# Moving the root spreads, the decay sums and their exponentials among the projection tiles of a two-layer hybrid trunk, and waiting for a bank at the third Z tile alone

## What is computed

```python
z = h @ w_in                       # one combined projection, split into
qa, ka, va, ub, vb, qkvc, bc, ac, zc, gates = jnp.split(z, split_idx, axis=-1)
o_b = chunk_gmlp(gelu(ub), gelu(vb), ...)     # vb is RMS-normalised over its 512 columns
# mixer C, gated DeltaNet
q = l2norm(q) * DN_DK ** -0.5; k = l2norm(k)  # after a short conv and silu
g = -exp(a_log) * softplus(a_raw + dt_bias)
gc = cumsum(g)                                # in chunks of 64; exp(gc), exp(g_last - gc), exp(g_last)
o = rmsnorm(o_f + flip(o_r), norm_g) * silu(z)
```

## Time and profile before

| | |
|---|---|
| median of three runs | 1875.45 us (1870.96 to 1878.6) |
| the profiled execution's own time | 1871.67 us |
| its span, first to last instruction | 1869.8 us |
| granted TensorE clock over the span | 0.988 of full speed |
| PE busy | 1778.6 us, 95% of the span |
| DVE, ACT, POOL busy | 1001.0, 785.9, 257.8 us |

### The profile page before, as it was taken

How to read it: one execution, slowest core, us unless ns; L and a number is a source line. 1 busy time by engine, 2 the same in 40 slices (tenths; PEclk the granted TensorE clock), 3 DMA queues, 4 the chain that set the end, 5 groups by cost and what they waited for, 6 DMA issues and landing times.

```text
span 1869.8 us, 32342 instructions
## 1 busy us (share of the span) xinstructions
PE 1778.6 (95%) x14062; PEld 1496.6 (80%) x14062; DVE 1001.0 (54%) x1291; ACT 785.9 (42%) x1100; POOL 257.8 (14%) x222
## 2 busy tenths in 40 slices
PE   5999999999999999999999999999999999999994
PEld 4989788888878999888898788887977555557883
DVE  2866435444745444326964445544747534347885
ACT  3344722223435222225365522225355533336774
POOL 2610032142000000004500123330002000000001
PEclk9999999999999999999999999999999999999997
DMA  9651152124644334347631323126566989989993
GB/s 358 214 215 52 45 215 69 55 84 142 218 169 135 114 113 134 135 150 255 222 128 52 120 97 115 47 76 222 212 227 248 350 298 322 333 279 392 389 382 124
DMA packets 175095, 350.78 MB, mean 188 GB/s; under 512 B 5066, under 2 KB 60386, under 8 KB 174449
## 3 DMA queue, kind: packets, MB, share of 16 engines
q1 hardware_dynamic: 171168, 335.01, 50.3%
q0 software_dynamic: 3792, 13.80, 2.1%
HBM read 319.43 MB, written 29.36 MB: 187 GB/s over the span
## 4 chain that ended last, share of the span: by engine, by line
PE 78%; DMA 8%; DVE 6%; ACT 5%; issue 2%; SPq 1%; POOL 1%; POOLq 0%; DVEq 0%; ACTq 0%
PE bank L1763 6%; PE bank L1182 6%; PE bank L1184 5%; PE bank L1183 5%; PE bank L1739 4%; PE bank L1742 3%; PE bank L1740 3%; PE bank L1627 3%; PE bank L1625 3%; PE bank L1626 3%; PE bank L1220 3%; PE bank L1222 3%; PE bank L1221 3%; PE bank L1434 2%; DMA ring<-in_ada_w 2%
## 5 line engine op out<-in xcount | busy, mean ns | idle before, releaser
L1901 ACT ACTIVATE ring_split<-ring 128x1024 fp32r<-128x1024 f32 (+2 forms) x84 | 119.4, 1440 | 175.2 <-DMA ring<-in_ffn_w_up 100.1
L1184 PE MATMUL bank<-hT_hi,ring_split 128*128 128x384 f32 x576 | 193.1, 335 | 0.0
L2810 DVE TENSOR_TENSOR ring_split<-ring,ring_split 128x2048 fp32r<-128x2048 f32 (+1 forms) x28 | 73.8, 2670 | 141.4 <-ACT ring_split L1901 141.4
L1182 PE MATMUL bank<-hT_hi,ring_split 128*128 128x384 f32 x384 | 139.8, 364 | 0.9 <-ACT oT L1901 0.5
L1222 PE MATMUL bank<-ring_split,hT_hi 128*128 128x256 f32 x480 | 137.0, 285 | 0.0
L785 DVE TENSOR_TENSOR ring_split<-ring,w_upper_a 128x2048 fp32r<-128x2048 f32 (+2 forms) x54 | 96.0, 1814 | 65.9 <-PE bank L1763 43.1
L1183 PE MATMUL bank<-hT_lo,ring_split 128*128 128x384 f32 x384 | 128.3, 334 | 0.0
L1627 PE MATMUL bank<-hT_hi,ring_split 128*128 128x384 f32 x352 | 118.8, 337 | 0.0
L1625 PE MATMUL bank<-hT_hi,ring_split 128*128 128x384 f32 x352 | 117.6, 334 | 0.0
L1626 PE MATMUL bank<-hT_lo,ring_split 128*128 128x384 f32 x352 | 117.2, 333 | 0.0
L1988 ACT ACTIVATE gates<-bank 128x384 f32<-128x384 f32 (+1 forms) x60 | 30.8, 513 | 191.8 <-PE bank L1184 157.5
(11 more groups left out here) (444 smaller groups left out, 4388.0 us busy)
## 6 DMA issues: line engine op xcount, KB each, us to landing
ring<-in_w_in SPq DMA_DIRECT2D x28, 2048.0 KB, 9.1
ring<-in_ada_w SPq DMA_DIRECT2D x24, 2048.0 KB, 12.5
ring<-in_moe_w_down SPq DMA_DIRECT2D x18, 1536.0 KB, 7.9
ring<-in_moe_w_gate SPq DMA_DIRECT2D x26, 1024.0 KB, 8.0
ring<-in_moe_w_up SPq DMA_DIRECT2D x26, 1024.0 KB, 10.4
ring<-in_w_branch SPq DMA_DIRECT2D x8, 1536.0 KB, 13.2
ring<-in_ffn_w_gate SPq DMA_DIRECT2D x11, 1024.0 KB, 5.4
ring<-in_ffn_w_up SPq DMA_DIRECT2D x11, 1024.0 KB, 7.9
```

The source lines that it names most:

```text
L1182: mm(out, hi, hT_hi[:, k], start=k == 0, stop=False)
L1184: last = mm(out, lo, hT_hi[:, k], start=False, stop=k == KT - 1)
L1901: return go(out, in_, ACT.Copy)
```

## The change

Four edits to PE's list, with DVE's and ACT's lists reordered to fit:

1. The root spreads run in three groups: 0 to 2 ahead of block 5, 3 to 5 behind the first token tile of its first half, 6 and 7 behind the first token tile of its second half. DVE's multiplies are grouped alike: 0 to 2 where all eight were; 3 to 5 behind the head sums; 6 and 7 behind `lower_block` (6, 1).
2. The decay sums run between the two halves of block 6, no longer behind it. On ACT the three exponentials come ahead of the value tiles' evacuations, and each value tile is squared right behind its evacuation.
3. The wait for `s_or` at 6 is taken from the head of the Z tiles and made only ahead of the third (which uses bank 4).
4. Three fill matmuls are added ahead of the wait for `route_ok` 1, and five ahead of the wait for `ht_ev`.

```diff
-            def token_tiles(layer, n, i, between=None):
+            def token_tiles(layer, n, i, between=None, after=()):
...
+                        elif g == 0 and n == T_Z and t == NT - 1:
+                            wait(pe, "s_or", layer, 6)
...
+                        for step in [x for at, x in after if at == (g, t)]:
+                            step()
...
-                for j in range(8):
-                    if j >= 3:
-                        wait(pe, "qkn", layer, j - 1)
-                    r = HQ[j % DNH]
-                    mm(B[(2, 3, 7)[j % 3]][:, 0:COUT], ident[r, r.start:r.start + 1].to_broadcast([32, P]), dsq[r, j // DNH],
-                       start=True, stop=True).then_inc(S["dst"], 1)
-                token_tiles(layer, T_UV, 5)
-                token_tiles(layer, T_UV + 3, 6)
-
-                wait(pe, "g_ok", layer, 1)
-                wait(pe, "qkn", layer, 9)
-                for t in range(NT):
...
+                def spread(js):
+
+                    for j in js:
+                        if j >= 3:
+                            wait(pe, "qkn", layer, j - 1)
...
+                spread((0, 1, 2))
+                token_tiles(layer, T_UV, 5, None, (((0, 0), lambda: spread((3, 4, 5))), ((1, 0), lambda: spread((6, 7)))))
+                def decay_sums():
+
+                    wait(pe, "g_ok", layer, 1)
+                    wait(pe, "qkn", layer, 9)
+                    for t in range(NT):
...
+                token_tiles(layer, T_UV + 3, 6, decay_sums)
...
                 wait(pe, "proj_ev", layer, T_Z)
-                wait(pe, "s_or", layer, 6)
                 token_tiles(layer, T_Z, 13)
...
                     turn_h(0)
+                    keep_warm(2, 3)
                     pe.wait_ge(route_ok, 1)
...
+                    keep_warm(2, 5)
                     pe.wait_ge(ht_ev, 2 * NT)
...
-                for t in range(NT):
-                    evac(T_UV + 3 + t, vB[:, t], ACT.Gelu_apprx_tanh)
-                wait(act, "proj_ev", layer, T_UV + 6)
-                wait(act, "qkn", layer, 9)
-                for t in range(NT):
-                    link(go(gsc, vB[:, t], ACT.Square, accum_out=vss[:, t:t + 1]))
-                go(vss, vss, ACT.Sqrt, bias=eps1, scale=1.0 / 512).then_inc(S["v_rt"], 1)
                 wait(act, "gc_v", layer, 1)
                 go(edec, edec, ACT.Exp)
                 go(egl, egl, ACT.Exp)
                 go(eg, gcs, ACT.Exp).then_inc(S["gc_e"], 1)
+                wait(act, "qkn", layer, 9)
+                for t in range(NT):
+                    evac(T_UV + 3 + t, vB[:, t], ACT.Gelu_apprx_tanh)
+                    wait(act, "proj_ev", layer, T_UV + 4 + t)
+                    link(go(gsc, vB[:, t], ACT.Square, accum_out=vss[:, t:t + 1]))
+                go(vss, vss, ACT.Sqrt, bias=eps1, scale=1.0 / 512).then_inc(S["v_rt"], 1)
...
-                for j in range(8):
-                    wait(dve, "dst", layer, j + 2)
-                    v.tensor_tensor(cv[:, j], cv[:, j], B[(2, 3, 7)[j % 3]][:, 0:COUT], ALU.mult).then_inc(S["qkn"], 1)
-
+                def normed(js):
+
+                    for j in js:
+                        wait(dve, "dst", layer, j + 2)
+                        v.tensor_tensor(cv[:, j], cv[:, j], B[(2, 3, 7)[j % 3]][:, 0:COUT], ALU.mult).then_inc(S["qkn"], 1)
+
+                normed((0, 1, 2))
                 lower_block(5, 2)
                 lower_block(5, 3)
...
                 v.tensor_reduce(ass, asq.rearrange("p t (h d) -> p (t h) d", d=HD), AX.X, ALU.add).then_inc(S["a_ss"], 1)
+                normed((3, 4, 5))
...
                 lower_block(6, 0)
                 lower_block(6, 1)
+                normed((6, 7))
```

More of the change, by code:

```diff
@@ L1298, in _ @@
-                last.then_inc(S["gc_mm"], 1)
+                def spread(js):
+                    for j in js:
+                        if j >= 3:
+                            wait(pe, "qkn", layer, j - 1)
+                        r = HQ[j % DNH]
+                        mm(B[(2, 3, 7)[j % 3]][:, 0:COUT], ident[r, r.start:r.start + 1].to_broadcast([32, P]), dsq[r, j // DNH],
+                           start=True, stop=True).then_inc(S["dst"], 1)
+                spread((0, 1, 2))
+                token_tiles(layer, T_UV, 5, None, (((0, 0), lambda: spread((3, 4, 5))), ((1, 0), lambda: spread((6, 7)))))
@@ new lines, in decay_sums @@
+                def decay_sums():
+                    wait(pe, "g_ok", layer, 1)
+                    wait(pe, "qkn", layer, 9)
+                    for t in range(NT):
+                        c0 = 32 * t
+                        mm(B[7][:, c0:c0 + 4], inclU, gg[:, t, 0:4], start=True, stop=True)
+                        mm(B[7][:, c0 + 4:c0 + 8], inclL, gg[:, t, 4:8], start=True, stop=True)
+                        mm(B[7][:, c0 + 8:c0 + 16], same, gg[:, t], start=True, stop=True)
+                        last = mm(B[7][:, c0 + 16:c0 + 32], ones, gm[:, t].rearrange("p c n -> p (c n)"), start=True, stop=True)
+                    last.then_inc(S["gc_mm"], 1)
```

## The result

The changed kernel takes 1860.42 us, the median of six runs (1856.63 to 1864.24), against 1875.61 us (six runs, 1870.96 to 1878.6) for the kernel before, beside it on the same chip. The ratio is 0.9931, interval 0.9911 to 0.9951: 12.9 us less, 9.2 to 16.7 by the interval; the two medians are 15.2 us apart. The forecast was 10.3 less. So the changed kernel is faster, clear of no change: 0.7% by the ratio, 0.49% at the near end of the interval. The profiled execution took 1856.63 us, the lowest of the six.

What follows compares the result with a forecast made beforehand. PE was taken to bound the kernel (78% of the chain that ended last). Terms 5.1 + 2.1 - 0.5 + 5.8 = 12.5 us less, minus 2.2 for one clock fall, gave 10.3: 1875.45 - 10.3 = 1865 us, range 1858 to 1872.

Steps and rivals of the forecast that it cites:

- Spreads: Root spreads around block 5: 3.0 us for all eight against 5.28 in layer 0, 2.3 less; layer 1 1.5 less.
- The clock behind them: Tile matmuls behind layer 0's spreads: the low clock (0.51) goes, 2.2 us less; bounds 0 and 2.2.
- DVE's order: Reordered DVE blocks: `lower_block` (6, 1) ends near 163.8, PE arrives at 164.0; a stall of up to 0.5 a layer possible.
- The tail: Last value-tile evacuation to first `kvt` copy: 3.17 us less on ACT, against 2.6 more for decay sums ahead of the last tile.
- exponentials and a gelu table load fit: ACT in block 6: room for both between the decay sums' end (about 175.3) and the first value tile's (178).
- Attention's table load: Attention's first exponential needs a new load of 1.28 us: 0.25 later a layer, 0.5 in all; upper bound 1.28 a layer.
- Z tiles: Idle time before the first Z matmul (1.94 and 2.28) and layer 0's low clock (1.6) go: 5.8 us less.
- the rival that they absorb the gain: Branch weights come when they came, so the Z gain is lost: 4.5 us less in all, 1871; chance 0.06.
- Fills: Three and five fill matmuls inside the router stage's two waits: no gain; up to 0.3 us if the cover shrank.
- The decay sums' fall: Tile matmuls behind the decay sums meet a low clock, 2.2 us a fall; one fall in two layers likeliest.
- The sum: Whole kernel: 12.5 us less without new losses, 10.3 less with one clock fall.
- The slower rival: Blocks 5 and 6: the clock stays at 1.2 GHz until the stage ends, up to 39 us slower, 1915; chance 0.03.

Runs made afterwards that it cites:

- fills alone: The kernel before with only the eight fill matmuls of the router stage added; ratio 1.000 (0.9983 to 1.0017), twelve runs.
- ACT's old order: The changed kernel with the decay sums still inside block 6 but ACT's order of before; ratio 0.9954 (0.9939 to 0.9969), ten runs.
- one wait: The changed kernel with ACT's wait for the decay sums' matmuls moved behind the first value tile's evacuation; 1859.09 us, one run.

## Why the prediction was right, point by point

**Spreads.** Forecast 3.0 us for all eight, so 2.3 and 1.5 less. They take 2.66, and four gaps of 0.1 around the second and the third group: 3.05, so 2.2 and 1.5 less. Right.

**The clock behind them.** Forecast: the fall of layer 0, worth 2.2, goes. It went, and this is the firmest finding on the clock. The three profiles with the eight spreads in one piece (before, fills alone, spreads in one piece again) have the fall in four of six layers; the 11 with the groups apart have it in none of 22.

**DVE's order.** `lower_block` (6, 1) was to end at 163.8 by 0.2 us before PE came. It ended at 163.28, and PE has no idle time there: right. `lower_block` (6, 3) was to end near 173.2, before the first half plus the decay sums; it ended at 172.48, but only the sums keep PE from waiting for it. Where they were taken out from between the halves, PE stood there for 0.3 us. DVE's multiplies 3 to 5 ran at 151.05, far behind the spreads and in nobody's way.

**The tail.** Forecast 3.17 less and 2.6 more: 0.57 a layer, less 0.25 for attention's load. Measured 3.29 less and 2.68 more: 0.6 a layer, less 0.3. The version with the edit undone is 0.95 behind at the copies, because it has the wait for `lower_block` (6, 3) besides. The copy came 4.96 us earlier than before, counted from the first spread, in layer 0 (forecast 5.1) and 2.03 in layer 1 (forecast 2.1). The step "exponentials and a gelu table load fit" between 175.3 and 178 was wrong in its reading: the load did not run ahead (177.99), and the first evacuation came 1.28 late. It cost nothing only because the next two tiles give ACT 1.5 us of slack each.

**Attention's table load.** It ran from 198.28 to 199.56, and the exponential stands 1.26 behind the scores where it stood 1.00: 0.26 a layer for a forecast 0.25. No drain is seen: the ACTIVATE starts 1.29 after the load does. The estimate of 10.6 us for four more loads, worked out in the prediction from ScalarE: Activation LUTs of the Trainium skill (What ACT_TABLE_LOAD costs), did not come true: the two loads in attention cost 0.3 us each, the two of gelu nothing at the copies, and with the tail edit undone, without the four, the ratio is the same.

**Z tiles.** Forecast 5.8: 1.94 + 1.6 + 2.28. The two profiles before and after have 3.5 in layer 0 and about 2.3 in layer 1, the undone version 1.95 + 3.84. Right in each term, except that the fall belongs to neither layer: with the idle time it came in three of six layers (before, wait restored, fills alone), without it in none of 22. The loads of the branch weights moved along in layer 0 in full. In layer 1 the first of them took 8.94 us, where it took 7.97 in the kernel before and 7.78 with the wait restored; the rival that they absorb the gain was right by about 1 us. What lengthened the transfer was not tried.

**Fills.** "Nothing": right, in both directions. The sentence beside it, that no low clock was there to gain, was right only for the profile of before; a gather at low clock turned up in three others.

**The decay sums' fall.** One fall in two layers was taken as likeliest. The changed kernel's profile has none, yet over the six profiles with the sums inside block 6 (the changed kernel, spreads, Z wait and fills undone, ACT's old order, one wait) it came in 6 of 12 layers. Each cost 1.5 where the forecast had 2.2. The rate was right and the profile lucky by one fall. That page of the Trainium skill which calls the activity monitor's window free-running (TensorE: Matmul & The Clock Gate, Part 1) is borne out in so far: the same instructions in the same order meet it differently from one execution to the next. The two profiles of the version with the sums behind the transposes show it for one and the same kernel: the gather took 7.25 us in one and 5.62 in the other.

**The sum.** 12.5 without falls was reached at layer 1's Z end, where the shift was 12.78 - 0.34 = 12.4. What lies beyond it is the last stretch, which the prediction left as it was: it gave 3.2 more. The row of PE there, changed kernel:

```profile
1437.64 0.47 PE L1751 MATMUL bank<-w_upper_b,ehid_hi 128*128 128x512 f32 x1 [3.06 <-DVE ring_split L785]
```

In the kernel before the same wait was 3.71, and a fall followed; here the clock stayed at 1.00. Of the 14 profiles 11 have a fall in that stage (between 1428 and 1456), so its absence is taken as scatter of one profile, not a gain; the other two without it are those with the spreads in one piece and with the wait restored. So 3.2 of the 15.0 us between the two profiles are not the edit's. The medians, 15.2 apart, and the ratio's 12.9 leave it open how many falls are usual, for the interval of 9.2 to 16.7 holds 10.3 and 12.5 alike. The slower rival, a clock that stays at 1.2 GHz through blocks 5 and 6, never occurred: every fall behind the spreads or the decay sums was over within 5 us of the first tile matmul behind them.

## What to carry to other kernels

Price a fall of the clock as a chance times its size (here about one in two, 1.5 to 2.9 us) for each place where PE idles or paces itself, and count it over all profiles at hand: the changed kernel's one profile had none behind the decay sums, and five others with the sums there had six in ten layers. A small group of matmuls on PE's path should first be tried in place of fills or a wait that already stands elsewhere: behind the transposes the decay sums cost 2.3 us a layer less than in the block. Look also at what they covered where they stood: between the halves of block 6 they had hidden a wait of 0.3 us for DVE, which another part of the same change had made. And where a step frees the next engine earlier, change both sides or neither: with the sums moved and ACT's order kept, PE stood idle, and the copies came 2.3 us later than with neither.

## What the runs showed of the hardware

- ACT's table load (1.28 us) starts as soon as ACT is free if its ACTIVATE has one wait: 175.73, ahead of an evacuation at 179.15. With a second wait ahead of the same ACTIVATE it started at 177.99, when the tile was done. No further time was seen between a load and its function: 1.29 us from the load's start to the ACTIVATE's.
- Falls of the granted clock follow idle or narrow stretches by chance: behind the paced spreads in 4 of 6 layers, behind the decay sums in 6 of 12 inside block 6. With an idle time of 1.9 to 2.3 us ahead of the Z tiles it was 3 of 6. Dense tile matmuls behind groups of up to 0.95 us of spreads had none in 22. Behind the wait for the branch weights in layer 1 it was 7 of 9 with 1.6 to 3.3 us of idle time and none of 4 with 0.9 to 1.1.
- Fills do not hold the clock for certain: with a remaining idle of 0.56 behind five fills, the gather once took 7.25 us for 5.62.
